# The expert stage of a float32 decoder: experts in an order found at run time, second blocks on resident weights, no loop, earlier turns of the activations

## The chip, the cores and the metric

The program runs on one core of one Trainium2 chip. The metric is the device time of one execution in microseconds (us). The profile is one execution, and all positions below are us from the start of its span.

## The reference, cut to what matters

The reference is a stack of two decoder blocks and a third one with a mixture of experts at its end. The change touches only that last part:

```python
logits = (xt @ router_w + router_b)            # 512 tokens, 32 experts
top_logits, top_idx = lax.top_k(logits, TOP_K) # 4 experts for each token
gates = jax.nn.softmax(top_logits, axis=-1)
# the tokens of each expert, in blocks of MOE_BLOCK rows:
hmid = xt[tok] @ w_gu[e] + b_gu[e]             # 1024 -> 2048, float32
glu  = jnp.minimum(hmid[:, 0::2], SWIGLU_LIMIT)
lin  = jnp.clip(hmid[:, 1::2], -SWIGLU_LIMIT, SWIGLU_LIMIT)
act  = glu * jax.nn.sigmoid(SWIGLU_ALPHA * glu) * (lin + 1.0)
out  = act @ w_down[e] + b_down[e]             # 1024 -> 1024
y = sum over the 4 chosen experts of gate * out
```

## The kernel before

Each expert has six units of weights of 2 MB: units 0 to 3 are the up weights, units 4 and 5 the down weights. They are loaded from HBM by SyncE's queue (L4183) into a ring of eight slots; a load waits until the unit that held the slot has been used (`unit_used`). So at most eight units, one expert and a third, are on the chip.

An expert's block holds up to 128 tokens, and a block is computed in one of two ways, chosen at run time by the number of its tokens (`is_half`):

- a **half block** (up to 64 tokens): float32 products in which two groups of 64 rows share the array (`up_half` L3698, `down_half` L3726). The activations are turned (transposed) by `turn_act_half` (L3711) once both pairs of up units are done, and `save_act_half` copies them from PSUM.
- a **full block** (65 to 128 tokens). Expert 0 has a plain float32 form for it (`up`, `down`). All others have the **parted** form: unit 0 in float32 (L3900), then each quarter of units 1 to 5 split by ScalarE into a rounded part (L88) and by VectorE into the rest (L91), and three products (L3870, L3871, L3875). `down_and_turn_parted` does unit 4, then turns the second half of the activations; `down_parted` does unit 5.

`first_blocks` walks the 32 experts in the order of their numbers. Experts 0 to 3 are written out, experts 4 to 27 are a loop of six iterations of four experts (`Fori`, on SyncE, TensorE, VectorE and ScalarE alike), and experts 28 to 31 are written out again. TensorE's instructions of one expert are: the up products, half of the turning of the next expert's rows (L3590), the turning of activations, the other half of the rows, the down products, and `find_tokens` of a later expert (L3559, the last instruction of each expert but the last three). Rows of an expert's tokens are fetched by GpSimd (L3575).

Tokens beyond the 128th of an expert are an **extra block**. `find` and `fill` work out on VectorE which there are (up to 15), and `extra_blocks` runs them after the 32 experts, in a loop of 15 iterations in each of which the body is behind an `If`. The weights of the first extra block's expert are loaded at the end of `first_blocks` (L4194), those of a later one in the body before it (L4351). The normed tokens are loaded whole (L4354), gathered by products with a selection matrix (L3665), and the block runs in either form. Last, `combine_and_finish` gathers each token's four rows (L4666), adds them and normalises.

Of the kernel before, what the change touches and what calls it, by code (L numbers as in the profile page):

```python
# [5 lines left out]
ALU = mybir.AluOpType  # L6
# [1015 lines left out]
def mlp(k, i, gain, clear_rows=False):  # L1022
# [15 lines left out]
    with ExitStack() as ctx:  # L1038
# [19 lines left out]
        with k.block() as block:  # L1058
# [35 lines left out]
            def _(act):  # L1094
                if clear_rows:
                    act.wait_ge(k.pool_made.sem, k.pool_made.at(1))
                for n, (u, is_up, j) in enumerate(order):
                    k.round_unit(act, u + 1)
                    if clear_rows:
                        rows = k.rows[3 * n:min(3 * n + 3, BLOCKS)].rearrange("b p d -> p b d")  # L1100
                        act.dma_start(rows, zero[:, :, :].broadcast_to([P, rows.shape[1], D])).then_inc(k.rows_cleared, 16)
# [2362 lines left out]
BLOCKS = EXPERTS + MOST_EXTRA  # L3464
# [3 lines left out]
SLOTS = 8  # L3468

# [32 lines left out]
class Experts:  # L3502


    def __init__(self, k, name, tables, one_by_one):
# [6 lines left out]
        self.loaded = [signal(f"loaded{r}") for r in range(SLOTS)]  # L3512
        self.sel_ready = signal("sel_ready")
        self.index_full = signal("index_full")
        self.index_ready = signal("index_ready")
        self.fetched = [signal(f"rows_fetched{r}") for r in range(2)]
# [16 lines left out]
    def make_sel(self, dve, j, par):  # L3533
# [4 lines left out]
        for t in range(TT):  # L3538
            ins = dve.tensor_scalar(T.sel[:, par, t, :], T.iota[:, :], T.place[:, t, bass.ds(j, 1)], None, ALU.is_equal)
# [95 lines left out]
    def save_act(self, act, j):  # L3635
        k, T = self.k, self.tables
        act.wait_ge(self.act_turned, 2 * j + 2)
        act.activation(T.actT[:, :, :].rearrange("p (b f) s -> p b (f s)", b=2), k.psum[:, 4:6, :], ACT.Copy)\
           .then_inc(self.actT_ready, 2)
# [33 lines left out]
    def up(self, pe, j, home, xg, par):  # L3673

        k, T = self.k, self.tables
        for pair in range(2):
            for r in range(2):
                w = home.wait(pe, 2 * pair + r)
                for g in range(2):
# [4 lines left out]
                    for c in range(HALF_K):  # L3684
                        pe.matmul(bank, xg[:, HALF_K * r + c, :], w[:, c, g * 512:(g + 1) * 512],
                                  start=(r == 0 and c == 0), stop=False)
# [20 lines left out]
    def turn_act_half(self, pe, j):  # L3707
        k, T = self.k, self.tables
        pe.wait_ge(self.act_ready, 4 * j + 4)
        for i in range(4):  # L3710
            ins = pe.transpose(k.psum[:, 4, i * P:(i + 1) * P], T.act[:, i * P:(i + 1) * P], k.ident[:, :])  # L3711
        ins.then_inc(self.act_turned, 2)

    def wait_for_down(self, pe, j):
        pe.wait_ge(self.actT_ready, 2 * j + 2)
# [3 lines left out]
    def down_half(self, pe, j, home, par, parted=False):  # L3719
        k, T = self.k, self.tables  # L3720
        self.wait_for_down(pe, j)
        w = [home.wait(pe, 4), home.wait(pe, 5)]
        banks = [k.psum[64 * g:64 * g + 64, 6, :] for g in range(2)]
        for c in range(KT):
            for g in range(2):
                ins = pe.matmul(banks[g], T.actT[:, c, 0:HALF], w[c // HALF_K][:, c % HALF_K, g * 512:(g + 1) * 512],  # L3726
                                start=(c == 0), stop=False)
        if parted:
            ins.then_inc(self.quarter_used.sem, 2 * HALF_K)
        for g in range(2):  # L3730
            pe.matmul(banks[g], T.bias_ones[:, par, 0:HALF], T.down_parts[:, g * 512:(g + 1) * 512], start=False,
                      stop=True).then_inc(self.down_full, 1)
# [18 lines left out]
    def sigmoids_half(self, act, j):  # L3751
        T = self.tables
# [3 lines left out]

    def save_act_half(self, act, j, parted=False):

        k, T = self.k, self.tables
        act.wait_ge(self.act_turned, 2 * j + 2)  # L3760
        turned = k.psum[:, 4, :].rearrange("p (pair h g s) -> p pair g h s", pair=2, h=2, g=2)
        home = T.actT[:, :, :].rearrange("p (pair g h) s -> p pair g h s", pair=2, g=2)
        ins = act.activation(home[:, 0, :, :, 0:HALF], turned[:, 0], ACT.Copy)
        if parted:
            ins.then_inc(k.unit_rounded.sem, PARTED + 1)
        act.activation(home[:, 1, :, :, 0:HALF], turned[:, 1], ACT.Copy).then_inc(self.actT_ready, 2)  # L3766
# [21 lines left out]
    def down(self, pe, j, home, par):  # L3788
# [953 lines left out]
```

## Time and the profile before

| what | us |
|---|---|
| median of the runs of before (3) | 3099.51 (3095.38 to 3104.8) |
| the profiled execution's own time | 3098.87 |
| its span | 3097.1 |
| first up product of expert 0 to last down product of expert 31 | 1894.2 to 2948.2 |
| from there to the first gather of the combination | 2948.2 to 3056.6 |
| combination and output | 3056.6 to 3097.1 |

The first 1894 us are the blocks ahead of the experts and are not touched by the change, but for a longer clearing of the output rows and some constants. The three last lines of the table are the stages that it touches. An engine's busy time is the sum of its instructions; "idle before ... <- X" is the time that it sat idle ahead of an instruction and what released it, where "issue" is a wait that the profile ascribes to nothing.

### The profile page before, as it was taken

The page shows a single profiled execution, that of the slowest core. Times are in us where ns is not written, and L with a number is a line of the kernel's source. Part 1 is how long each engine was busy: PE and PEld are TensorE (multiplying, and loading weights), DVE is VectorE, ACT ScalarE, POOL GpSimd, SP SyncE. Part 2 cuts the span into 40 slices and gives each one's busy share as a digit, 9 for nine tenths or more (in the row PEclk, how much of TensorE's full clock was granted, in tenths as well). Part 3 has the DMA queues.
Part 4 walks back from the last instruction along what each step waited for, and adds up shares of the span by engine and source line. Part 5 has one row for each costly group of instructions (what it writes and reads, how often), then busy time and mean ns, then how long its engine had stood idle before and what let it go on. Part 6 is the DMA issues. An engine that isn't in the chain of part 4 may idle for free. (4 is left out here: it accounts for less than half of the span.)

```text
span 3097.1 us, 35668 instructions
## 1 busy us (share of the span) xinstructions
PE 2741.5 (89%) x13162; PEld 1970.5 (64%) x13163; DVE 1614.4 (52%) x2447; ACT 1047.0 (34%) x1464; POOL 193.8 (6%) x213
## 2 busy tenths in 40 slices
PE   7877999999999899999966876998989998899962
PEld 6655778888878788888754663553655455455530
DVE  4864545444555544446855536652855454464413
ACT  4444443322224432233333231330634233343301
POOL 0530000000000000000012130000000000000002
PEclk9988999999999999999976787999999999999986
DMA  3110314444233132322210038999999999999974
GB/s 131 58 51 28 109 62 177 171 169 183 101 120 111 66 116 82 109 82 71 103 60 1 1 122 329 404 414 414 413 385 380 361 412 370 414 412 395 415 291 151
DMA packets 192096, 638.46 MB, mean 206 GB/s; under 512 B 12413, under 2 KB 18204, under 8 KB 191522
## 3 DMA queue, kind: packets, MB, share of 16 engines
q1 hardware_dynamic: 173856, 579.61, 48.7%
q10 hardware_dynamic: 11106, 39.11, 3.2%
q0 software_dynamic: 6912, 16.68, 1.4%
q8 instruction: 151, 2.47, 0.3%
q14 instruction: 71, 0.58, 0.1%
HBM read 600.61 MB, written 43.25 MB: 208 GB/s over the span
## 5 line engine op out<-in xcount | busy, mean ns | idle before, releaser
L91 DVE TENSOR_TENSOR unit_low<-unit_whole,unit_high 128x4096 fp32r<-128x4096 f32 (+3 forms) x95 | 287.8, 3035 | 174.8 <-ACT unit_high L88 172.9
L669 PE MATMUL psum<-tokens_high,unit_high 128*128 128x512 f32 (+2 forms) x1016 | 372.5, 367 | 4.4 <-PEq L865 1.6
L669 PE MATMUL psum<-tokens_high,unit_low 128*128 128x512 f32 (+2 forms) x1016 | 368.7, 363 | 0.0
L669 PE MATMUL psum<-tokens_low,unit_high 128*128 128x512 f32 (+2 forms) x1016 | 368.6, 363 | 0.0
L88 ACT ACTIVATE unit_high<-unit_whole 128x4096 fp32r<-128x4096 f32 (+2 forms) x65 | 225.8, 3474 | 374.2 <-PE psum L669 291.3
L91 DVE TENSOR_TENSOR moe_low<-ring_slot,moe_w_high 128x1024 fp32r<-128x1024 f32 x228 | 266.7, 1219 | 19.4 <-ACT moe_w_high L88 18.4
L88 ACT ACTIVATE moe_w_high<-ring_slot 128x1024 fp32r<-128x1024 f32 x228 | 236.5, 1055 | 61.4 <-PE psum L3875 60.4
L3698 PE MATMUL psum<-ring_slot,hT 128*64 128x512 f32 x1136 | 251.9, 594 | 0.0
L669 PEld LDWEIGHTS psum<-tokens_high,unit_high 128*128 128x128 f32 (+1 forms) x1016 | 191.0, 188 | 37.9 <-DVE unit_low L91 4.0
L669 PEld LDWEIGHTS psum<-tokens_low,unit_high 128*128 128x128 f32 (+1 forms) x1016 | 191.1, 188 | 31.6 <-issue 1.6
L669 PEld LDWEIGHTS psum<-tokens_high,unit_low 128*128 128x128 f32 (+1 forms) x1016 | 191.0, 188 | 30.6 <-issue 0.2
L669 PE MATMUL psum<-unit_high,hidden_high 128*128 128x512 f32 x512 | 199.7, 390 | 0.0
L669 PE MATMUL psum<-unit_high,hidden_low 128*128 128x512 f32 x512 | 199.4, 389 | 0.0
L669 PE MATMUL psum<-unit_low,hidden_high 128*128 128x512 f32 x512 | 199.4, 389 | 0.0
L3741 DVE TENSOR_SCALAR moe_glu<-psum 128x256 f32<-128x256 f32 x42 | 17.8, 425 | 324.4 <-PE psum L3704 232.7
L3698 PEld LDWEIGHTS psum<-ring_slot,hT 128*64 128x64 f32 x1136 | 83.5, 137 | 148.9 <-issue 147.7
L3726 PE MATMUL psum<-ring_slot,moe_actT 128*64 128x512 f32 x640 | 155.8, 641 | 9.7 <-ACT moe_actT L3766 9.7
L1147 DVE TENSOR_TENSOR x_residual<-psum,x_residual 128x512 f32<-128x512 f32 x128 | 84.4, 687 | 117.7 <-PE psum L669 117.7
L3870 PE MATMUL psum<-moe_w_high,moe_xg_high 128*128 128x512 f32 x312 | 131.1, 420 | 0.0
L3755 ACT ACTIVATE moe_sig<-moe_glu 128x256 f32<-128x256 f32 x42 | 17.5, 416 | 316.0 <-DVE moe_glu L3741 316.0
L3871 PE MATMUL psum<-moe_low,moe_xg_high 128*128 128x512 f32 x312 | 122.1, 391 | 0.0
L1137 DVE SCALAR_TENSOR_TENSOR hT<-psum,hidden_relu 128x512 f32<-128x512 f32 x64 | 43.8, 689 | 147.3 <-ACT hidden_relu L1109 147.3
(646 smaller groups left out, 4908.9 us busy)
## 6 DMA issues: line engine op xcount, KB each, us to landing
ring_slot<-in_moe_w_gu SPq DMA_DIRECT2D x118, 2048.0 KB, 19.4
ring_slot<-in_moe_w_down SPq DMA_DIRECT2D x60, 2048.0 KB, 20.5
unit_whole<-in_moe_w_gu SPq DMA_DIRECT2D x18, 2048.0 KB, 16.9
unit_whole<-in_w_up SPq DMA_DIRECT2D x16, 2048.0 KB, 7.5
unit_whole<-in_w_down SPq DMA_DIRECT2D x16, 2048.0 KB, 7.7
expert_rows<-zero_row ACTq DMA_DIRECT2D x15, 1536.0 KB, 5.3
unit_whole<-in_moe_w_down SPq DMA_DIRECT2D x8, 2048.0 KB, 19.7
unit_whole<-in_w_in SPq DMA_DIRECT2D x5, 2048.0 KB, 7.7
```

Of the source, the lines that this page charges most:

```text
L88: return act.activation(self.high, self.whole, ACT.Copy)
L91: return dve.tensor_tensor(self.low, self.whole, self.high.bitcast(F32), ALU.subtract)
L669: ins = pe.matmul(bank, a, c, start=(first and m == 0), stop=(last and m == len(parts) - 1))
L1137: dve.scalar_tensor_tensor(out=hidden[j % 2].whole[:, b, :], in0=bank, scalar=0.0, in1=relu[:, h % 2, :], op0=ALU.max, op1=ALU.mult)\
L1147: dve.tensor_tensor(x, bank, x, ALU.add).then_inc(k.bank_free.sem, 1)
L3698: ins = pe.matmul(banks[g], xg[:, c, 0:HALF], w[c // HALF_K][:, c % HALF_K, g * 512:(g + 1) * 512], start=(c == 0), stop=False)
L3726: ins = pe.matmul(banks[g], T.actT[:, c, 0:HALF], w[c // HALF_K][:, c % HALF_K, g * 512:(g + 1) * 512], start=(c == 0), stop=False)
L3741: dve.tensor_scalar(T.glu[:, pair, :], bank[:, :, 0], 7.0, None, ALU.min).then_inc(self.glu_ready, 2)
L3755: act.activation(T.sig[:, pair, :], T.glu[:, pair, :], ACT.Sigmoid, scale=1.702).then_inc(self.gate_ready, 2)
L3870: pe.matmul(banks[g], a.high[:, f, :], w.high[:, cols], start=(first and q == 0), stop=False)
L3871: pe.matmul(banks[g], a.high[:, f, :], w.low[:, cols], start=False, stop=False)
```

## The change

1. **An order found at run time.** `put_in_order` ranks the experts by their counts of tokens on VectorE: experts 0 and 1 stay first and second, the others are taken by `RANKS`, rank 0 being the most loaded one. There are 34 steps: expert 0, expert 1, rank 0, rank 0's second block, rank 26, then twelve pairs of ranks (2, 14), (3, 15) to (13, 25), then rank 1, rank 1's second block, and ranks 27, 28, 29.
2. **Second blocks with resident weights.** The two most loaded experts are computed twice in a row on one load of their weights (steps 2 and 3, steps 29 and 30). All four of these steps have, for a full block, the plain float32 form ("whole"). What is left over stays with `extra_blocks`, which now loads weights and tokens inside its body only.
3. **No loop.** All 34 steps are written out on every engine; an expert's number and the column of its places are read from a table into registers.
4. **Turns.** In a half block the first pair of activations is turned inside the second pair's up products and copied at once; the second pair is turned between the down products of unit 4 and of unit 5. In the parted form the second half is turned ahead of the last quarter of unit 4, not behind it. Both halves of the next expert's rows are turned together after the up products.

The diff's core:

```diff
+STEPS = EXPERTS + SECONDS            # 32 + 2
+AT_SECOND = (3, STEPS - 4)
+FIRST = 2
+RANKS = [EXPERTS - 2, EXPERTS - 1, 0, 0, 26] + [r for m in range(12) for r in (2 + m, 14 + m)] + [1, 1, 27, 28, 29]
+def in_steps(step):
+    for q, b, kind in ((0, 0, "first"), (1, 1, "parted"), (2, 2, "whole"), (3, 2, "whole"), (4, 3, "parted")):
+        step(Step(q, 0, b, kind))
+    for i in range(1, ROUND_LAST):
+        for b in range(PER_ROUND):
+            step(Step(PER_ROUND * i + b + 1, i, b, "parted"))
+    for q, b, kind in ((0, 0, "whole"), (1, 0, "whole"), (2, 1, "parted"), (3, 2, "parted"), (4, 3, "parted")):
+        step(Step(STEPS - 5 + q, ROUND_LAST, b, kind))
...
     def up_half(self, pe, j, home, xg, par, parted=False):
...
             for c in range(KT):
+                if pair == 1 and c == HALF_K:
+                    self.turn_act_half(pe, j, 0)
...
+        for pair in range(2):                       # down_half
+            if pair == 0:
+                self.wait_for_down(pe, j, 1)
+            else:
+                self.turn_act_half(pe, j, 1)
+                if finds:
+                    self.find_tokens(pe, j + 3, 1 - par)
+                pe.matmul(banks[0], T.bias_ones[:, par, 0:HALF], T.down_parts[:, 0:512], start=False, stop=False)
+                pe.wait_ge(self.actT_ready, 2 * j + 2)
...
     def down_and_turn_parted(self, pe, j, home):
...
-        self.unit_products(pe, j, 4, home, self.banks(6), self.tables.act_parts, True, self.act_low_at(j, 0))
+        self.unit_products(pe, j, 4, home, banks, parts, True, self.act_low_at(j, 0), range(HALF_K - 1))
         self.turn_act_pair(pe, j, 1)
+        self.unit_products(pe, j, 4, home, banks, parts, True, None, range(HALF_K - 1, HALF_K))
...
             for q in range(HALF_K):                 # activate_parted
+                if pair == 1 and q == HALF_K // 2:
+                    split_act(pair)
                 self.split_quarter(dve, j, n + 1, q, home)
-            split_act(pair)
+            if pair == 0:
+                split_act(pair)
...
+    def put_in_order(self, dve):
...
+        step(dve.tensor_tensor(more, keys.unsqueeze(1).broadcast_to([P, EXPERTS, EXPERTS]),
+                               keys.unsqueeze(2).broadcast_to([P, EXPERTS, EXPERTS]), ALU.is_gt))
+        step(dve.reduce_sum(T.rank[:, :], more, AX))
+        for i, of in enumerate((T.ids, T.counts)):
+            step(dve.tensor_tensor(here, T.rank[:, :].unsqueeze(1).broadcast_to([P, STEPS, EXPERTS]),
+                                   T.ranks[:, :].unsqueeze(2).broadcast_to([P, STEPS, EXPERTS]), ALU.is_equal))
+            step(dve.tensor_tensor(here, here, of[:, :].unsqueeze(1).broadcast_to([P, STEPS, EXPERTS]), ALU.mult))
+            step(dve.reduce_sum(T.by_step[:, i, :], here, AX))
...
+            def load(home, q, used_by):             # first_blocks, SyncE
+                e = expert_at(sp, q)
+                for n in range(PER_EXPERT):
+                    by = used_by[0 if n < 2 else 1]
+                    if by is not None:
+                        used(by, (n - 2) % PER_EXPERT)
+                    sp.dma_start(ring_view(k, home.slot(n)), expert_unit(k, e, n)).then_inc(E.loaded[home.slot(n)], 16)
...
+            load(Home(E, 0, 3), 4, (1, 3))
+            load(Home(E, 0, 4), 5, (3, 4))
...
             E.save_tokens(dve, 1)                   # first_blocks, VectorE
-            E.make_sel(dve, 2, 0)
             E.make_bias(dve, 0, 0)
+            E.make_bias(dve, 1, 1)
+            extras.put_in_order(dve)
             E.save_gather(dve, 0, 0, 0)
             E.save_gather(dve, 0, 1, 0)
+            E.make_sel(dve, 2, 0, column_at(dve, 2))
+            E.make_sel(dve, 3, 1, column_at(dve, 3))
             extras.find(dve)
             extras.find_jumps(dve)
-            in_rounds(dve, step)
+            in_steps(step)
...
             def body(b):                            # extra_blocks, SyncE
+                e = expert_of(sp, b)
+                sp.wait_ge(block_free, b + 1)
+                sp.dma_start(T.y, k.y_rows.rearrange("(t p) d -> p t d", p=P)).then_inc(y_loaded, 16)
+                for n in range(PER_EXPERT):
+                    sp.dma_start(ring_view(k, n), expert_unit(k, e, n)).then_inc(E.loaded[n], 16)
```

## Rows read from the trace of the kernel before

**Rows 1.** Two stages: length, PE, PEld, DVE, ACT, POOL busy, clock, DMA share, GB/s

```profile
1894.20:2948.20 1054.00, 972.05 (x4328) 541.18 (x4328) 566.20 (x913) 375.85 (x464) 32.56 (x30) 0.97 1.00 397
2948.20:3056.60 108.40, 64.36 (x342) 33.79 (x340) 11.40 (x30) 6.94 (x16) 0.00 (x0) 0.84 0.48 191
```

**Rows 2.** Timeline of TensorE, ScalarE and GpSimd after expert 31

```profile
2947.88 0.39 PE L3731 MATMUL psum<-moe_down_bias_parts,moe_bias_ones 128*64 128x512 bf16 x2
2969.85 9.18 PE L3665 MATMUL psum<-moe_sel_whole,ring_slot 128*128 128x128 f32 x64 [21.58 <-issue]
3043.73 0.38 PE L3731 MATMUL psum<-moe_down_bias_parts,moe_bias_ones 128*64 128x512 bf16 x2
3048.48 0.20 ACT L4407 ACTIVATE moe_store_seen<-ones 128x1 f32<-128x1 f32 x1 [3.09 <-DMA expert_rows<-moe_o]
3056.64 0.96 POOL L4666 DMA_INDIRECT unit_whole<-expert_rows,moe_row  x1 [189.49 <-PEq L4660]
```

**Rows 3.** DMA issues from 1780 on: KB each, median us to landing

```profile
ring_slot<-in_moe_w_down SPq DMA_DIRECT2D x60, 2048.0 KB, 20.5
unit_whole<-in_moe_w_down SPq DMA_DIRECT2D x8, 2048.0 KB, 19.7
expert_rows<-moe_o ACTq DMA_DIRECT2D x13, 512.0 KB, 7.8
expert_rows<-moe_o ACTq DMA_DIRECT2D x21, 256.0 KB, 6.3
```

**Rows 4.** Windows of four experts' steps (columns as in rows 1)

```profile
2046.40:2086.70 40.30, 38.45 (x164) 27.53 (x163) 32.40 (x39) 25.13 (x27) 1.23 (x1) 1.00 1.03 415
2855.70:2881.00 25.30, 23.36 (x120) 8.47 (x118) 4.78 (x13) 2.67 (x6) 0.99 (x1) 1.00 1.03 413
...
2278.50:2325.10 46.60, 40.95 (x164) 28.60 (x163) 32.62 (x39) 25.02 (x27) 1.23 (x1) 0.93 0.96 373
2391.00:2431.30 40.30, 38.44 (x164) 27.63 (x163) 32.63 (x39) 24.91 (x27) 1.23 (x1) 1.00 0.92 352
```

**Rows 5.** Waits of TensorE, 1890 to 2950: us in total, times, longest

```profile
PE psum L3711 <- DVE moe_act L3748: 32.3, 19, 2.7
PE psum L3875 <- DVE moe_actT_low L3944: 11.8, 13, 1.0
PE psum L3870 <- ACT moe_actT_high L3979: 11.7, 13, 0.9
...
PE psum L3900 <- issue: 11.2, 3, 3.8
PE psum L3726 <- ACT moe_actT L3766: 9.3, 18, 0.8
PE psum L3698 <- issue: 5.6, 2, 3.8
```

**Rows 6.** Timeline of TensorE: at a loop's edge, and between written-out experts

```profile
2282.42 9.64 PE L3900 MATMUL psum<-unit_whole,hT 128*128 128x512 f32 x16 [3.69 <-issue]
...
2881.10 7.13 PE L3900 MATMUL psum<-ring_slot,hT 128*128 128x512 f32 x16
```

**Rows 7.** Timeline of TensorE: first float32 unit of a full block

```profile
2046.51 7.11 PE L3900 MATMUL psum<-ring_slot,hT 128*128 128x512 f32 x16
2053.36 0.50 PE L3870 MATMUL psum<-moe_w_high,moe_xg_high 128*128 128x512 f32 x1
```

**Rows 8.** Timeline of VectorE around the first expert

```profile
1891.35 0.69 DVE L3605 TENSOR_TENSOR hT<-psum,feature_vectors 128x512 f32<-128x512 f32 x1 [11.19 <-PE psum L3590]
...
1894.74 1.66 DVE L4103 TENSOR_TENSOR extra_pick<-extra_order,moe_nth 128x1440 f32<-128x1440 f32 x1
...
1906.51 0.19 DVE L4131 TENSOR_TENSOR head_gains<-extra_order,moe_ids 128x32 f32<-128x32 f32 x1
...
1908.54 0.43 DVE L3741 TENSOR_SCALAR moe_glu<-psum 128x256 f32<-128x256 f32 x1 [1.13 <-issue]
...
1937.29 0.42 DVE L3741 TENSOR_SCALAR moe_glu<-psum 128x256 f32<-128x256 f32 x1 [0.86 <-DVE moe_row L4150]
```

More of the change, by code:

```diff
@@ L3796, in down @@
                 for c in range(HALF_K):
-                    pe.matmul(bank, T.actT[:, HALF_K * r + c, :], w[:, c, cols], start=(r == 0 and c == 0), stop=False)
+                    ins = pe.matmul(bank, T.actT[:, HALF_K * r + c, :], w[:, c, cols], start=(r == 0 and c == 0), stop=False)
+                if counted and r == 1 and half == 1:
+                    ins.then_inc(self.quarter_used.sem, 2 * HALF_K)
                 if r == 1:
@@ L4097, in find @@
         step(ins)
+        step(dve.scalar_tensor_tensor(out=self.flag[:, 0, :], in0=T.rank[:, :], scalar=float(SECONDS), in1=self.flag[:, 0, :],
+                                      op0=ALU.is_ge, op1=ALU.mult))
         dve.memset(self.zero[:, :], 0.0)
@@ L4204, in _, with step @@
             pool.wait_ge(T.y_stored, 16 * TT)
-            for j in range(EXPERTS):
-                E.fetch_rows(pool, j)
+            for q in range(STEPS):
+                E.fetch_rows(pool, q)
         @block.tensor
         def _(pe):
-            def step(i, b, j, first, last):
-                half = is_half(pe, j)
-                home = Home(E, i, b)
-                par = b % 2
+            def step(s):
+                if s.q == FIRST:
+                    pe.wait_ge(extras.ordered, 1)
+                half = is_half(pe, s)
+                q, home, par = s.q, s.home(E), s.par
@@ L4214, in step @@
                 xg = T.xg[:, par]
[L4215 to L4216 removed]
+                counted = s.kind != "first"
                 with pe.If(half):
[L4219 to L4220 removed]
+                    E.wait_for_up(pe, q)
+                    E.up_half(pe, q, home, xg, par, counted)
                 with pe.Else():
[L4222 to L4223 removed]
@@ L4226, in step @@
                 with pe.If(half):
-                    E.turn_act_half(pe, j)
+                    E.down_half(pe, q, home, par, counted, s.has(3))
                 with pe.Else():
-                    if parted:
-                        E.down_and_turn_parted(pe, j, home)
-                    else:
-                        E.turn_act(pe, j)
-                if following:
-                    E.turn_rows(pe, j + 1, 1, 1 - par, saved=j + 3 if not (last and b == PER_ROUND - 2) else EXPERTS)
-                with pe.If(half):
-                    E.down_half(pe, j, home, par, parted)
@@ L4237, in step @@
-                with pe.Else():
-                    if parted:
-                        E.down_parted(pe, j, home, par)
-                    else:
-                        E.down(pe, j, home, par)
-                if not (last and b >= 1):
-                    E.find_tokens(pe, j + 3, 1 - par)
+                    if s.kind == "parted":
+                        E.down_and_turn_parted(pe, q, home)
+                        E.down_parted(pe, q, home, par)
+                    else:
+                        E.turn_act(pe, q)
+                        E.down(pe, q, home, par, counted)
@@ L4295, in _, with step @@
+            extras.put_in_order(dve)
             E.save_gather(dve, 0, 0, 0)
             E.save_gather(dve, 0, 1, 0)
-            E.make_sel(dve, 3, 1)
-            E.make_bias(dve, 1, 1)
+            E.make_sel(dve, 2, 0, column_at(dve, 2))
+            E.make_sel(dve, 3, 1, column_at(dve, 3))
             extras.find(dve)
             extras.find_jumps(dve)
-            in_rounds(dve, step)
+            in_steps(step)
         @block.scalar
         def _(act):
-            def step(i, b, j, first, last):
-                parted = not (first and b == 0)
-                xg = T.xg[:, b % 2]
-                if first and b == 1:
+            def step(s):
+                q = s.q
+                if q == 1:
```

363 lines of the change are left out of this document (208 added, 155 removed).

## The prediction

> **What bounds the kernel now.** I read the windows first. From the first up product to the last down product the 32 experts take 1054.0 us, at 397 GB/s and a DMA share of 1.00; then the extra blocks take 108.4 us at 191 GB/s and half the DMA share [rows 1]. So there are two things to look at: a stage in which TensorE (972 us busy) and the DMA are both nearly full, and one in which neither is.
>
> The DMA issues tell how many blocks there are: 68 loads of down weights are 34 experts' loads, and the stores are 13 of 512 KB (full blocks) and 21 of 256 KB (half blocks), 34 blocks [rows 3]. So there are two extra blocks. Both are half: the down bias rows that close them and expert 31 are L3731, the half form [rows 2]. An expert with over 256 tokens would have a full extra block, so the two belong to two experts, each with 129 to 192 tokens: exactly the two that `AT_SECOND` takes. Of the 32 first blocks 13 are full and 19 half, experts 0 and 1 among the latter (L3741 is the half form) [rows 8]. By rank the full ones are 0 to 12.
>
> The single steps come next. A half block takes 25.3 us, of which TensorE is busy 23.4; a parted one 40.3, busy 38.5 [rows 4]. A load of an expert is 12.58 MB; where the DMA is full it moves 412 to 415 GB/s [rows 4], so 5.05 us for a unit and 30.3 for an expert. Half blocks are thus bounded by the DMA and parted ones by TensorE, and the ring evens out an expert and a third at most. In the same row list the step at 2391 moved only 352 GB/s: a parted block behind a parted one leaves the DMA idle. Last, the waits: TensorE waits in each half block for the activations (32.3 us in 19) and their copy (9.3), and in each parted one twice, 0.9 us each (11.7 and 11.8 in 13) [rows 5]. And it waits five times 3.4 us in mean (11.2 + 5.6), up to 3.8, for "issue" ahead of the first up product [rows 5], once at 2282.4, where sixteen products then take 9.64 us in place of 7.1 [rows 6, 7]. The five places are the experts 8, 12, 16, 20 and 24, the loop's back edges; the written-out experts (29 to 30, at 2881.10) have no such gap [rows 6].
>
> **The extra blocks go.** Both are done as second blocks, and the count of extra blocks becomes 0. From the last down product at 2948.2 the combination's first gather now comes 108.4 us later [rows 1]. What must stay: the copies and the store of the last block, some 5 us (3043.73 + 0.4 to 3048.48), and the walk through an empty loop; 13 empty iterations and the block's end take 8.2 us (3048.48 to 3056.64), so 15 take 9.4 [rows 2]. With 1.5 for two more block borders the tail is 16 us: **92 saved**. The reload of the residual, 2 MB or 5 us, lies beside it.
>
> **The start gets longer.** `put_in_order` stands on VectorE ahead of the first gather's copy. Two passes over 1024 elements and six over 1088: a pass over 1440 takes 1.66 [rows 8], so I scale to 1.22 and 1.29, together 10.2. Some eleven small ones of 0.1 to 0.2 and two register loads of 1.1 (the gap ahead of L3741 [rows 8]) make 14.4. VectorE idled 11.2 us there [rows 8]; less what is moved, the copy comes 2.5 late, and two register loads and the selections now behind it make the first up product 4.5 late. But VectorE is late from then on: `find` with six more small steps ends 7 us later, so the first activation comes at about 1915.4 and not at 1908.5. TensorE now stops for it in the middle of the second pair's up products (the new turn), and the half pair, activation, and down products still follow: step 0 ends 10 us later. The same again in step 1: `fill` and `find_rows` held the activation until 1937.3 [rows 8]; now until about 1950, and TensorE has 16 us of work left behind it. Step 2 starts at 1966 and not 1952: **14 lost**. If the pauses were hidden this would be 0; it can hardly be more than 20.
>
> **Shorter steps.** In a half block, turning the first pair inside the up products and the second between the down units takes away the two waits, (32.3 + 9.3) / 19 = 2.2 less some rest: 23.5. In a parted block the turned half has a quarter (1.4 us) to hide behind: 40.3 less 1.8 = 38.5. If nothing is won the steps stay 25.6 and 40.3. The back edges (five times 3.4 and up to 2.5 of slow products behind each [rows 6], together some 25 us) go.
>
> **Whole blocks.** Rank 0 and rank 1 lose the parted form. Sixteen records of float32 take 6.85 us (2046.51 to 2053.36) [rows 7], 0.43 each; a whole block has 64 up and 32 down, 41.1 us; six bias products 1.3, turns and tokens 2.0, the last activation, copy and borders 3.5: **48 us**, twice.
>
> **The pairs, and the DMA's holes.** A pair of a parted and a half step is 62 us for TensorE. For the DMA it is two loads, a store of 0.52 and one of 0.26 MB, and 0.6 MB of rows: 26.6 MB, or 64.2 us at 414 GB/s. So after the change the DMA is the bound of the pairs, and the shorter steps are worth little by themselves. And it gets two holes. The ring lets it bring two units of the next expert while a whole block runs (10 us), then nothing until the second block frees its first pair, 7 us into it. I walk it step by step:
> - step 2, 1966 to 2014; step 3 frees its first units at 2021. The DMA has been idle since about 1976.
> - from there the DMA is never without a free slot (I followed slots and landings for steps 3 to 9: each slot is free 3 to 10 us before the DMA comes to it). Until the second unit of step 29 it brings 150 units, 314.6 MB, with 6.3 of rows and 9.4 of stores 330 MB, **800 us** at 413. TensorE would need 16.4 + 23.5 + 11 x 38.5 + 13 x 23.5 = 769; it waits the other 31.
> - step 29 (whole), 2821 to 2869.
> - steps 30 to 33, half, 23.5 each and bound by the loads after the hole: units 2 to 5 of step 31 and twelve more from 7 us on, sixteen of 5.05 and the last down products, **97 us**. End of the last down product 2966.
>
> That is 18 later than 2948.2. With the tail of 16: the first gather at 2982 for 3056.6, **75 us** saved. On the profiled execution's 3098.87 (its span is 3097.1, and it stands 0.6 below the median of the runs shown) this gives 3024.
>
> **A rule on the DMA's rate.** The full windows moved at most 415 GB/s [rows 4]. The Trainium skill, page "DMA: Bandwidth & Descriptors", section "Bandwidth", has 425 GB/s for a 16 MB load; by that the long stretch would be 777 us in place of 800 and the sum 3001. No row here reaches it.
>
> **Rivals.**
> - *TensorE stays the bound: the turns win nothing.* For it: the waits may only move, to ScalarE's copy behind its roundings. Then steps 3 to 28 take 18 + 25.6 + 11 x 40.3 + 13 x 25.6 = 820 for 800, steps 31 to 33 another 2, and the time is 3046. Against: the waits lie where the change puts work, and VectorE is busy only 32 of 40 us in a parted step [rows 4].
> - *The order costs nothing* (VectorE's idle 11 us take it and TensorE's pauses shrink): 3010.
> - *The holes are wider*: the DMA also misses time in the pairs, or idle TensorE is granted a lower clock (0.93 in the step with a pause, 1.00 without [rows 4]) and a parted step takes 42 for 38.5. That would be up to 11 x 3.5 = 39 less the 31 of slack, and 2 us a pair of lost transfer on top: 3050 to 3080.
> - *Slower: the written-out steps stop as the back edges do.* Every step now jumps over the arm that it does not take. If that cost the 3.7 us of a back edge and the 2.5 of slow products behind it [rows 6], 34 steps cost 211, less the 31 of slack: 3204. It decides from 3.1 us a step on. Against: before, experts 0 to 3 and 28 to 31 jump over the same arms, with no gap [rows 6]. The Trainium skill, page "Runtime: NRT & Kernel Launch", section "Instruction fetch mechanics", says that a taken branch to outside the fetched window waits for a fetch; by that rule the back edges' gaps are explained, and the jumps would pay only if an arm were longer than the window.
> - *The change doesn't do what it says*: an extra block is left. The rows exclude it for these inputs.
>
> **How the numbers follow.** Forecast (3008 to 3040) 0.62; turns without gain (3040 to 3050) 0.14; order free and faster DMA (under 3008) 0.06; wider holes (3050 to 3080) 0.12; slower 0.04; the rest 0.02 near no change. The range reaches from 3008, the free order, to 3056, the turns without gain and some of the wider holes: about 0.8. A measurement of this kernel tells 0.3% (9 us) from no change. Faster 0.94, same 0.02, slower 0.04.
>
> **What would show it.** No product of the gather L3665 and no wait of 20 us ahead of the combination; 66 down loads become 64; VectorE's order for some 14 us before the first copy; step 2 at 1966; whole blocks of 48 us with the DMA idle for over 35 us in the first; pairs of 64 us at 412 to 415 GB/s, with half steps of 23.5 where nothing waits; no 3.7 us gaps. The prediction falls if the pairs take over 67 us, or the tail over 25.

## The result, and the profile after

| what | before, us | after, us |
|---|---|---|
| median (4 runs each) | 3098.27 (3095.38 to 3104.8) | 3062.72 (3055.36 to 3066.16) |
| profiled execution's own time, span | 3098.87, 3097.1 | 3055.36, 3053.3 |

The ratio is 0.9874 (0.9848 to 0.99): 35.6 us or 1.3% faster, where 3024 had been forecast with a range of 3008 to 3056. The direction was right, and the gain was half of what I had said. The profiled execution is the fastest of its four; it stands 31 us above the forecast, and the median another 7.4.

The windows of the changed kernel by stage: length, PE, PEld, DVE, ACT, POOL busy, clock, DMA share, GB/s (as [rows 1]):

```profile
1894.00:1961.00 67.00, 54.11 (x236) 21.76 (x236) 46.49 (x113) 5.76 (x12) 1.98 (x2) 0.89 0.83 325
1977.00:2017.20 40.20, 37.95 (x119) 16.62 (x119) 8.91 (x33) 3.11 (x6) 0.00 (x0) 0.96 0.04 15
2017.20:2838.70 821.50, 786.30 (x3521) 436.05 (x3517) 443.58 (x700) 319.43 (x401) 28.42 (x26) 0.99 1.02 408
2853.00:2895.00 42.00, 39.75 (x125) 17.42 (x125) 6.95 (x20) 3.53 (x7) 0.13 (x1) 0.96 0.27 105
2895.00:2991.20 96.20, 89.57 (x418) 37.13 (x414) 17.34 (x47) 10.33 (x26) 1.98 (x2) 0.98 0.90 361
2991.20:3013.30 22.10, 0.01 (x1) 0.00 (x0) 0.00 (x0) 1.39 (x3) 0.00 (x0) 0.58 0.32 109
```

The first row is steps 0 and 1. The second and fourth are the DMA's two holes, beside the two experts whose weights stay: TensorE is busy, the DMA moves 15 GB/s in the first and 105 in the second, which it fills for a quarter. Between them the DMA is full for 821.5 us. In the last row TensorE does nothing and the DMA brings 2.4 MB, the residual for the most part; this stage was 108.4 us before [rows 1].

The timeline of VectorE has the new order ahead of the first gather's copy (L3638), with two small gaps of "issue" where registers are loaded:

```profile
1877.38 1.23 DVE L4165 TENSOR_TENSOR extra_prod<-extra_order 128x1024 f32<-128x1024 f32 x1
1878.64 1.22 DVE L4167 TENSOR_REDUCE moe_rank<-extra_prod 128x32 f32<-128x1024 f32 x1
1879.89 1.29 DVE L4169 TENSOR_TENSOR extra_prod<-moe_rank,moe_ranks 128x1088 f32<-128x1088 f32 x1
...
1889.74 0.17 DVE L4187 TENSOR_SCALAR moe_place<-moe_place 128x4 f32 x1 [1.04 <-issue]
1890.49 0.17 DVE L4187 TENSOR_SCALAR moe_place<-moe_place 128x4 f32 x1 [0.57 <-issue]
1890.70 1.29 DVE L3638 TENSOR_TENSOR hT<-psum,feature_vectors 128x512 f32<-128x512 f32 x2
```

TensorE's timeline shows what that does: in steps 0 and 1 the turn of the first pair (L3751) stops for an activation that VectorE is late with. The third row is the start of step 2, the fourth that of step 29:

```profile
1912.91 0.69 PE L3751 MATMUL psum<-ident,moe_act 128*128 128x128 f32 x2 [5.74 <-DVE moe_act L3796]
1945.39 0.69 PE L3751 MATMUL psum<-ident,moe_act 128*128 128x128 f32 x2 [6.97 <-DVE moe_act L3796]
1961.13 10.57 PE L3721 MATMUL psum<-ring_slot,hT 128*128 128x512 f32 x24
...
2838.66 7.10 PE L3721 MATMUL psum<-unit_whole,hT 128*128 128x512 f32 x16 [0.61 <-issue]
```

SyncE's timeline has the holes: four loads whose issue takes 61.6 us because the last two wait for step 3 to free the first pair, and nothing between the loads at 2843.56 and at 2894.84:

```profile
1956.68 61.60 SPq L4295 DMA_DIRECT2D ring_slot<-in_moe_w_gu  x4
...
2843.56 9.15 SPq L4295 DMA_DIRECT2D ring_slot<-in_moe_w_gu  x2
2894.84 0.37 SPq L4295 DMA_DIRECT2D unit_whole<-in_moe_w_gu  x1
```

The end, on TensorE, ScalarE and GpSimd (as [rows 2]): last down product, store seen, first gather of the combination:

```profile
2990.83 0.38 PE L3780 MATMUL psum<-moe_down_bias_parts,moe_bias_ones 128*64 128x512 bf16 x1
2995.75 0.20 ACT L4519 ACTIVATE moe_store_seen<-ones 128x1 f32<-128x1 f32 x1 [3.23 <-DMA expert_rows<-moe_o]
3013.32 0.96 POOL L4779 DMA_INDIRECT unit_whole<-expert_rows,moe_row  x1 [90.47 <-PEq L4773]
```

The walk from 2995.75 to 3013.32 does no work at all: 15 rounds of the loop of extra blocks, each with nothing in it. It took 17.6 us, where 13 such rounds had taken 8.2 [rows 2].

And the rate of the long stretch, in three windows of 64 us of the same view:

```profile
2058.00:2122.00 64.00, 63.63 (x285) 36.47 (x283) 37.95 (x56) 28.80 (x36) 2.22 (x2) 1.00 1.03 414
2378.00:2442.00 64.00, 63.12 (x283) 36.40 (x285) 37.97 (x56) 28.45 (x36) 2.22 (x2) 1.00 1.02 409
2570.00:2634.00 64.00, 60.92 (x274) 35.49 (x270) 37.16 (x55) 28.05 (x34) 2.22 (x2) 1.00 1.02 405
```

At a full DMA share it falls from 414 to 405 GB/s. That was in no row of before on which I had built.

### The profile page after: what moved, and what is told of

Read it like the earlier page. It is cut to its first block and busy times, and to the rows that moved or that the text cites. A ratio compares the mean times of both kernels' runs of the same rounds, so it can differ in the third digit from the quotient of the medians.

```text
span 3053.3 us, 34265 instructions
## 1 busy us (share of the span) xinstructions
PE 2739.2 (90%) x12978; PEld 1934.9 (63%) x12979; DVE 1575.4 (52%) x2449; ACT 1011.2 (33%) x1445; POOL 196.6 (6%) x249
## 5 line engine op out<-in xcount | busy, mean ns | idle before, releaser
L3738 PE MATMUL psum<-ring_slot,hT 128*64 128x512 f32 x1184 | 274.6, 611 | 15.3 <-DMA ring_slot<-in_moe_w_gu 15.3
L91 DVE TENSOR_TENSOR moe_low<-ring_slot,moe_w_high 128x1024 fp32r<-128x1024 f32 x200 | 233.2, 1218 | 4.0 <-ACT moe_w_high L88 3.9
L88 ACT ACTIVATE moe_w_high<-ring_slot 128x1024 fp32r<-128x1024 f32 x200 | 208.2, 1057 | 44.0 <-PE psum L3922 42.7
L3789 DVE TENSOR_SCALAR moe_glu<-psum 128x256 f32<-128x256 f32 x42 | 17.8, 425 | 354.7 <-PE psum L3744 259.3
L3738 PEld LDWEIGHTS psum<-ring_slot,hT 128*64 128x64 f32 x1184 | 95.6, 140 | 163.2 <-issue 151.1
L3774 PE MATMUL psum<-ring_slot,moe_actT 128*64 128x512 f32 x624 | 145.9, 610 | 16.3 <-issue 14.7
L3917 PE MATMUL psum<-moe_w_high,moe_xg_high 128*128 128x512 f32 x264 | 108.2, 410 | 2.9 <-DVE moe_low L91 2.8
L660 PE MATMUL psum<-unit_high,high_parts 128*128 128x512 f32 (+2 forms) x256 | 99.5, 389 | 10.5 <-DVE low_parts L1997 4.1
L669 PEld LDWEIGHTS psum<-unit_high,hidden_high 128*128 128x128 f32 x512 | 96.1, 188 | 19.9
## 6 DMA issues: line engine op xcount, KB each, us to landing
unit_whole<-in_moe_w_gu SPq DMA_DIRECT2D x16, 2048.0 KB, 24.3
```

What stands on the lines that cost most here:

```text
L88: return act.activation(self.high, self.whole, ACT.Copy)
L91: return dve.tensor_tensor(self.low, self.whole, self.high.bitcast(F32), ALU.subtract)
L660: ins = pe.matmul(bank, a, c, start=(i == 0 and m == 0), stop=(i == len(products) - 1 and m == len(parts) - 1))
L669: ins = pe.matmul(bank, a, c, start=(first and m == 0), stop=(last and m == len(parts) - 1))
L3738: ins = pe.matmul(banks[g], xg[:, c, 0:HALF], w[c // HALF_K][:, c % HALF_K, g * 512:(g + 1) * 512], start=(c == 0), stop=False)
L3774: ins = pe.matmul(banks[g], T.actT[:, HALF_K * pair + c, 0:HALF], w[pair][:, c, g * 512:(g + 1) * 512], start=(pair == 0 and c == 0), stop ...
```

## The experiments

All are edits of the changed kernel. "H" in an expectation is the theory that the DMA and its holes set the pace, "P" the rival that TensorE's steps do. Medians are of 4 to 10 executions. Executions of the same code differ by 10 to 15 us (3055.36 to 3066.16 for the changed kernel, 3052.13 to 3067.38 in run 11), so beside the medians I compare positions in the profiles, above all that of the last down product: 2990.83 in the first profile of the changed kernel, 2995.58 in its second (run 11).

**1. The place of the second hole's weights.** The two blocks of each of the two most loaded experts change places: the half-full second block comes first, and the full one behind it, now in the parted form, which frees its units one by one.

```diff
-AT_SECOND = (3, STEPS - 4)
+AT_SECOND = (2, STEPS - 5)
...
-(3, 2, "whole")    # and (1, 0, "whole") at the end
+(3, 2, "parted")   # and (1, 0, "parted")
```

> The changed kernel with the two blocks of the most loaded experts in the other order: the second block (half) first, then the first block, which can then take the parted form and frees its units one after another. Theory H (the stage goes at the pace of the DMA, plus the time in which no slot is free): the time without transfers behind step 2 falls from some 40 us to 15 and that behind step 29 from some 31 to 5, so about 50 us less than the changed kernel's 3063: 3012. Rival P (TensorE's steps set the pace): only the two whole blocks become parted ones, 2 x (49 - 38.6) = 21 less: 3042.

Measured: 3028.02, ratio 0.9769 (0.9748 to 0.9791), 35 us less than the change as made. That lies in the middle between H (3012) and P (3042) and decides for neither. SyncE's timeline does more. The four loads at the first hole are now issued in 42.4 us in place of 61.6, and at the second hole no load is issued for 23.9 us (2835.54 to 2859.45) in place of 42.1:

```profile
1957.27 42.40 SPq L4295 DMA_DIRECT2D ring_slot<-in_moe_w_gu  x4
...
2825.76 9.78 SPq L4295 DMA_DIRECT2D ring_slot<-in_moe_w_gu  x2
2859.45 0.37 SPq L4295 DMA_DIRECT2D unit_whole<-in_moe_w_gu  x1
```

Of the 19.2 us at the first hole 17.8 are kept at the loads ahead of the second (2825.76 for 2843.56): this hole was paid almost in full, though TensorE is busy beside it, as H has it; P would give some 10. The last down product comes at 2963.58 for 2990.83, 27.3 us earlier, so of the 18.2 us at the second hole only some 9.5 are kept. That is what P gives for one block (48.8 - 38.6): behind it the last three half steps take 72.9 us in place of 79.6, 24.3 each, TensorE's own pace. The median's 35 holds besides the 7.4 us by which the changed kernel's median stands above its profiled execution.

**2. The order.** Parted experts first, then the half ones.

```diff
-+ [r for m in range(12) for r in (2 + m, 14 + m)] +
++ list(range(2, 26)) +
```

> The changed kernel with the 24 middle steps sorted by count (eleven parted ones, then thirteen half ones) and not paired. Theory H: in each parted step behind a parted one the DMA idles some 5 us, and the half steps then run at the DMA's pace of 32 us each; the stretch takes about 11 x 38.6 + 13 x 32 = 841 against 785 for the same steps paired: 50 us more, 3113. Rival P: the sum of TensorE's steps is the same, so 3063.

Measured: 3094.72, ratio 0.9986 (0.9972 to 1.0001): 32 us worse than in pairs. Its windows say why. With parted steps alone TensorE has not one idle us and the DMA brings 354 GB/s; with half steps alone TensorE is busy 207 of 256 us, at 412:

```profile
2186.00:2442.00 256.00, 256.00 (x1099) 185.94 (x1098) 218.64 (x266) 166.70 (x182) 8.59 (x7) 1.00 0.97 354
2570.00:2826.00 256.00, 207.28 (x944) 76.53 (x942) 44.83 (x136) 23.01 (x56) 7.91 (x8) 0.95 1.02 412
```

The pairing is thus worth about as much as the whole change. The parted steps also show that a DMA share near 1 (0.97) does not mean a full rate: with 354 GB/s the engines count as busy.

**3. Fewer bytes.** In steps 4 to 28 only one row of each block is stored; 9.4 MB of stores are left out, and the output lacks those rows.

```diff
-dma_start(self.rows_of(block, HALF), T.o[0:HALF, :])
+dma_start(self.rows_of(block, 1 if few else HALF), T.o[0:1 if few else HALF, :])
```

> The changed kernel storing only one row of each block in steps 4 to 28 (it leaves out the rest of these stores, 9.4 MB). Theory H: 9.4 MB at 408 GB/s are 23 us less, 3040; and if the stores are also what takes the rate from 414 to 405 GB/s in the later pairs, another 12 less, 3028, with 414 in all windows. Rival P: nothing changes, 3063.

Measured: 3035.56, ratio 0.9802 (0.9777 to 0.9827): 27 us less, 26 of them in steps 2 to 28 of the profile (851.6 us for 877.5). At 413 GB/s the bytes are 23. No work of TensorE was taken away, so with the new turns the DMA is the bound of the stretch. Its rate still fell, to 404 to 410 from 2378 on: the stores are not the cause of the fall.

**4. The old turns.** Turning of activations as before, in both forms; the edit puts back the old `down_half`, `turn_act_half` and `down_and_turn_parted`, and the copies and splits that go with them.

```diff
-                if pair == 1 and c == HALF_K:
-                    self.turn_act_half(pe, j, 0)
...
-        self.unit_products(pe, j, 4, home, banks, parts, True, self.act_low_at(j, 0), range(HALF_K - 1))
+        self.unit_products(pe, j, 4, home, self.banks(6), self.tables.act_parts, True, self.act_low_at(j, 0))
         self.turn_act_pair(pe, j, 1)
-        self.unit_products(pe, j, 4, home, banks, parts, True, None, range(HALF_K - 1, HALF_K))
```

> The changed kernel with the turns of the activations and of the next rows where the kernel before had them. Theory H: the shorter steps lie inside the DMA's pace; only steps 0, 1, 3, 4 and 30 to 33 show them, a few us, and steps 0 and 1 no longer stop in the middle of the up products: 3060 to 3072. Rival P: eleven parted steps of +1.8 and twenty half steps of +2 us: +60, 3120.

Measured: 3065.91, ratio 0.9885 (0.9861 to 0.9909): 3 us above the change, which is within the scatter. But that is a difference of two larger ones. With the old turns step 2 starts at 1954.74, 6.4 us before that of the changed kernel (1961.13; 11.8 before its second profile), and step 29 at 2848.32, 9.7 us behind it (2838.66):

```profile
2848.32 7.11 PE L3721 MATMUL psum<-unit_whole,hT 128*128 128x512 f32 x16
```

So steps 2 to 28 take 893.6 us in place of 877.5 (875.0 in the second profile), 16 to 19 more, and the DMA's rate over the long stretch is 400 GB/s and not 408: TensorE was the slower of the two there. The new turns save this time and give back 6 to 12 us of it at the start, where the turn inside the up products waits for a late VectorE. TensorE's waits in the long stretch, first with the old turns, then in the changed kernel:

```profile
PE psum L3749 <- DVE moe_act L3786: 23.5, 15, 1.6
PE psum L3915 <- DVE moe_actT_low L3984: 10.9, 11, 1.0
PE psum L3910 <- ACT moe_actT_high L4019: 8.4, 11, 0.8
PE psum L3764 <- ACT moe_actT L3804: 4.7, 14, 0.4
```

```profile
PE psum L3774 <- issue: 17.0, 9, 3.0
PE psum L3738 <- DMA ring_slot<-in_moe_w_gu: 11.0, 5, 3.3
PE psum L3917 <- DVE moe_low L91: 2.8, 8, 0.7
```

47.5 us of waits for turned activations are gone, and 31 of other waits have come. 11.0 of them are for weights by name. The 17.0 of "issue" at L3774, ahead of the first down product of a half step, have no releaser in the trace. They are likely waits for the down weights: with fewer bytes (run 3) 3.5 us of them are left, and no half step before 2233 has one, though each has the same jump. That was not shown further.

**5. The start.** `find` and `fill` are spread over VectorE's time in steps 0 to 2, and `find_rows` over steps 4 to 10.

```diff
-            extras.find(dve)          # ahead of step 0
-            extras.find_jumps(dve)
...
+                    extras.find(dve)                      # after step 0
+                elif s.q == 1:
+                    extras.find_jumps(dve)
+                    extras.fill(dve, 0)
+                    extras.fill(dve, 1)
```

> The changed kernel with the search for extra blocks taken off the start: find after step 0, find_jumps and half of fill after step 1, the rest after step 2, find_rows in steps 4, 6, 8 and 10. If VectorE's lateness in steps 0 and 1 is what costs there (TensorE stops 5.7 and 7.0 us in the middle of the up products), step 2 starts at 1948 and not at 1961, and 13 us are kept to the end: 3050. Rival: the first weights arrive no sooner (units 2 to 5 of step 1 and of step 2 wait for used units anyway), and less than 4 us are won.

Measured: 3044.8, ratio 0.9827 (0.9806 to 0.9848): 18 us less. Step 2 starts at 1944.61 in place of 1961.13, 16.5 us earlier, and the DMA's first hole ends as much earlier (2001.75 for 2018.28). At the last down product 11.4 are left (2979.45 for 2990.83; 16.1 against the second profile), so most of it reaches the end, not all. The edit also gives step 1 the whole form for a full block; expert 1 has a half block and doesn't take that arm.

**6. The empty loop.** It is put behind one test of its count.

```diff
-            with eng.Fori(0, MOST_EXTRA) as b:
-                with eng.If(b < count):
-                    body(b)
+            with eng.If(count > 0):
+                with eng.Fori(0, MOST_EXTRA) as b:
+                    ...
```

> The changed kernel with the whole loop over extra blocks behind one more If on their count. The tail was forecast at 16 us and took 22.1. If it is the walk through fifteen empty iterations (some 1.1 us each), it falls to about 7 and the time by 15: 3048. Rival: it is the borders of the blocks and the store, and 3 us at most are won.

Measured: 3044.33, ratio 0.9819 (0.9797 to 0.9841): 18 us less. From the store seen to the first gather it is now 7.3 us, 10.3 less than in the first profile of the changed kernel and 17.8 less than in its second:

```profile
3000.59 0.20 ACT L4520 ACTIVATE moe_store_seen<-ones 128x1 f32<-128x1 f32 x1 [3.20 <-DMA expert_rows<-moe_o]
...
3007.85 0.96 POOL L4780 DMA_INDIRECT unit_whole<-expert_rows,moe_row  x1 [81.93 <-PEq L4774]
```

**7. The loop again.** Steps 5 to 28 as a loop of six iterations of four steps, on all four engines.

```diff
-    for i in range(1, ROUND_LAST):
+    with eng.Fori(1, ROUND_LAST) as i:
```

> The changed kernel with its steps 5 to 28 as a loop of six iterations again, on all four engines. Theory H: five back edges of some 6 us on TensorE lie within the DMA's pace for the most part (TensorE had 20 to 30 us of slack over the stretch): 3063 to 3073. Rival P: they add in full, 27 to 30 us: 3091.

Measured: 3087.48, ratio 0.9968 (0.9955 to 0.998): 25 us worse. My theory, that the DMA's slack takes the back edges, fell. TensorE waits five times for some 10 us at the back edges, with slow products behind (8.7 to 10.0 us for sixteen in place of 7.1), and five times for 1.0 to 1.3 us ahead of the parted step between:

```profile
2200.47 9.98 PE L3948 MATMUL psum<-unit_whole,hT 128*128 128x512 f32 x16 [10.37 <-issue]
```

```profile
PE psum L3948 <- issue: 56.4, 10, 10.4
```

The slow products are TensorE's clock: from 2200.5 to 2204 the granted clock is 0.50, the lower of its two levels (1.2 and 2.4 GHz), after 10 us in which it did nothing; from 2210 on it is 1.00 again. The 9.64 us of [rows 6] are the same, 0.50 from 2282.5 to 2286.5. 56.4 us of stops cost 25. Before, five such places had 16.8 in all [rows 5]; why a back edge takes 10 us in this loop of four steps and took 3.7 in that of four experts [rows 6], no run tells.

**8. The three together** (1, 5 and 6).

> Second block ahead of the first (as in the run before), late find and skipped empty loop together. By theory H they add up, since each takes away a time in which nothing is transferred: 3028 - 13 - 15 = 3000.

Measured: 3004.67 (3003.43 to 3005.08), ratio 0.9695 (0.9674 to 0.9716). It is 58 us below the change as made and beats both kernels. Alone they gave 35, 18 and 18, which is 13 more. In the profiles there is no overlap: the last down product comes 27.3 and 11.4 us earlier in runs 1 and 5 and 39.5 in this one (2951.33), and the walk through the empty loop falls from 17.6 to 6.8. The 13 fit the scatter: each single gain is counted from a median that stands 7.4 above the profiled execution, three times in the sum and once in the 58, which makes 15.

**9 to 11. Where the rate falls.** One kernel reads the weights of one expert for all steps but the first (the products are then with expert 5's weights); one takes the pairs in reverse; one is the changed kernel once more.

```diff
-                e = expert_at(sp, q)
+                e = 5
```

```diff
-[r for m in range(12) for r in (2 + m, 14 + m)]
+[r for m in range(12) for r in (13 - m, 25 - m)]
```

> The changed kernel with every weight load of the 34 steps reading the same expert's weights (expert 5), so all loads read one 12 MB stretch; each expert's tokens are multiplied by expert 5's weights, so the output is another one. Question: from about 2378 us on, the changed kernel's transfers moved 404 to 409 GB/s at a DMA share of 1.02, where the first five windows of 64 us moved 413 to 415. Theory A (the place read in memory: some experts' weights are read slower): all windows read alike, 412 to 415 throughout or one low value throughout; at 414 the long stretch of 821 us takes 12 us less and the median is about 3050. Theory B (what is mixed with the loads at that time, or the time in the run): the fall stays in the same windows, and the median is within 4 us of 3063.

> The changed kernel with its twelve pairs of parted and half steps taken in reverse, ranks 13 and 25 first and ranks 2 and 14 last; the same bytes and the same products. Theory A (the place read): the slow windows, 404 to 409 GB/s, move to the front of the stretch, 2058 to about 2500, and 413 to 415 come last; median within 4 us of 3063. Theory B (time or neighbours in time): 413 to 415 stay first, 404 to 409 stay last; the same median. The order of the pairs itself is worth nothing by either, since each pair moves 24 MB and needs 63 us of products.

> The changed kernel unaltered, once more, to stand beside the two others on the same chip and to give its windows a second time. Expected: a median within 4 us of 3062.7, and the fall of the rate from 413 to 415 down to 404 to 409 GB/s in the same windows, from about 2378 us on; if the fall is a chance of one execution, the windows differ by more than 3 GB/s from the first profile.

Measured: 3055.71, ratio 0.9867 (0.9846 to 0.9888); 3057.69, 0.9868 (0.9852 to 0.9885); 3061.07, 0.9868 (0.9847 to 0.9889). The fall is in the same windows in all three, from 2378 on (410 from 2314 on with the reversed pairs): 402 to 411 GB/s, 413 to 415 before but for 412 in one. The window from 2570 on:

```profile
2570.00:2634.00 64.00, 60.33 (x269) 35.59 (x272) 37.49 (x55) 28.05 (x34) 2.21 (x2) 1.00 1.02 405
```

```profile
2570.00:2634.00 64.00, 61.85 (x271) 35.80 (x270) 36.52 (x51) 28.06 (x34) 2.21 (x2) 0.98 1.02 404
```

The first is of the one expert, the second of the reversed pairs. Neither the place read nor the order is the cause. Loads that wait for a free slot are not the cause either: in the changed kernel the up units took 24.5 to 25.5 us from issue to landing in the windows from 2058 to 2186, and 24.2 to 26.0 from 2378 to 2698; where the queue runs short it is some 10 (the parted steps of run 2). The profile of the kernel run once more differs from the first in two places: the last down product comes 4.8 us later, and the walk through the empty loop took 25.1 us and not 17.6:

```profile
3000.53 0.20 ACT L4519 ACTIVATE moe_store_seen<-ones 128x1 f32<-128x1 f32 x1 [3.26 <-DMA expert_rows<-moe_o]
...
3025.63 0.96 POOL L4779 DMA_INDIRECT unit_whole<-expert_rows,moe_row  x1 [100.00 <-PEq L4773]
```

**12. A pause.** SyncE waits twice, ahead of the loads of steps 14 and 22, until the load before has landed.

```diff
+                    if b == 0 and i in (3, 5):
+                        Home(E, i, 0).wait(sp, PER_EXPERT - 1)
                     load(Home(E, i, b + 1), ...)
```

> The changed kernel, where SyncE waits twice, ahead of the loads of steps 14 and 22 (about 2330 and 2590 us), until the load before them has landed, so that the queue of loads runs empty once and then fills again with all freed units at once. Theory C (the rate of the loads falls with how long the queue has been full without a break, as the 16 DMA engines drift apart, and a pause sets it back): one slice of low rate at each place, then 413 to 415 GB/s for the next 200 us or more; each pause costs about 2 to 3 us of transfers and the higher rate gives back about 2% of 250 us, so that the median is 0 to 8 us below 3061. Theory B2 (the rate falls with the time in the run, whatever the queue did before): 404 to 409 GB/s in the windows from 2442 us on in spite of the pauses, and the median 2 to 10 us above 3061.

Measured: 3063.53, ratio 0.9883 (0.9859 to 0.9906). The rate is back at once, in the windows behind each pause:

```profile
2314.00:2378.00 64.00, 59.23 (x259) 34.62 (x257) 35.96 (x50) 27.58 (x32) 2.22 (x2) 0.97 0.89 348
2378.00:2442.00 64.00, 61.65 (x278) 35.72 (x276) 38.86 (x59) 28.03 (x34) 2.21 (x2) 1.00 1.03 415
...
2570.00:2634.00 64.00, 57.34 (x248) 34.01 (x248) 37.51 (x55) 27.65 (x33) 2.22 (x2) 0.96 0.90 356
2634.00:2698.00 64.00, 61.74 (x266) 35.76 (x264) 36.45 (x51) 27.65 (x33) 1.23 (x1) 0.96 1.03 413
```

So the rate depends on how long the queue has been full without a break, and not on the time in the run. The price of a pause was mis-sized: not 2 to 3 us of transfers but (414 - 348) / 414 and (414 - 356) / 414 of 64 us, 10 and 9. The shape of a draining queue hints at a cause. It stands in 40 slices of the DMA's busy tenths: the changed kernel at its first hole (slices of 1 us), behind steps 0 and 1 in which it was not full (share 0.83), the kernel with pauses (slices of 1.6 us), after some 300 us at full share, and the changed kernel at its second hole (slices of 1 us), after 821.5 us at full share:

```profile
DMA  9999999999999999970310000000000000000000
```

```profile
DMA  9999999999987536310199999999999999999999
```

```profile
DMA  9999999999842221100000000000000000000007
```

The first queue ends within 4 us, the second fades over some 11, the third over some 8. One reading is that the 16 DMA engines drift apart, and that a load counts as landed only when the last one has done its part. It stays a guess: the engines were not measured one by one, the fade after 821.5 us is no longer than that after 300, and fewer loads stood in the first queue (landing 15.2 us after issue, for some 25 in the others), which is a rival that no run separates. The pauses gave back 13 to 16 of their 19 us (step 29 comes at 2845.1, for 2838.7 and 2841.6 in the two profiles of the changed kernel) and won nothing in the median.

## Why the prediction was wrong in size, point by point

Against the profiled execution (31 us off) and with what the others showed:

- **Extra blocks go, 92 saved: right in kind, the tail mis-sized.** The tail is 22.1 us and not 16. The failing step was "15 take 9.4": I scaled the walk through the empty loop from 13 rounds behind the last full one. It measured 17.6 in this execution and 25.1 in the second profile, 7.3 with the loop skipped. In the eleven profiles that have this loop it is either 17.6 to 18.8 (seven) or 24.9 to 25.1 (four), so the tail is 6 or 14 us over my figure.
- **The start, 14 lost: right, 9 to 15 measured.** Step 2 at 1961.1 and 1966.6 in the two profiles, for 1966, by the mechanism named (the first turn stops for a late activation). Run 4 parts it: with the order but the old turns step 2 comes at 1954.7, so the order costs some 3 us and the turn inside the up products the rest. What I had not said is that it could be undone: run 5 moved VectorE's search and won 11 to 16 us at the last down product, 18 in the median.
- **Shorter steps: right on the steps, and the rival priced well what they bring.** Steps 3, 4 and 5 take 24.0, 24.1 and 38.6 us, for 23.5 and 38.5. The rival in which the turns win nothing set steps 3 to 28 at 20 us more; the old turns took 16 to 19 more in steps 2 to 28 (run 4). The 3 us of run 4's median are what is left after the loss at the start. That the shorter steps are "worth little by themselves" was too low.
- **Whole blocks, 48: right.** 1961.1 to 2010.1 is 49.0; step 29 took 48.8.
- **The holes: right in size, the first paid almost in full, the second for half.** The DMA stands nearly still from 1977 to 2017.2, and no load is issued for 42 us at the second. Run 1 shortened them by 19.2 and 18.2 us and kept 17.8 and 9.5.
- **The long stretch, 800 us: the step that failed most, 21.5 us.** "At 413" was the rate of windows behind pauses; the mean of the unbroken stretch was 408, which is 10 us. Before, the loop's edges and parted steps in a row (373 and 352 GB/s [rows 4]) had let the queue run short again and again, so its rows never showed the low rate of a queue that stays full. The rest is bytes: the DMA moved 335.6 MB for the 330 that I counted. 3.3 MB of the difference are weights (317.9 for 314.6, units under way at the window's end), 0.8 rows (7.1 for 6.3), and 1.2 are instructions, which I had left out. The Trainium skill, page "DMA: Bandwidth & Descriptors", section "Bandwidth", gives 425 GB/s for a 16 MB load; by that the stretch would have been still shorter. The trace disagrees twice, with 415 at most and 404 in the lowest window.
- **The last four steps, 97: 103.7.** I counted sixteen units of 5.05 and left out the rows and stores beside them: 34.7 MB went in that window, 84 us at 413 and not 81, and the ring's start gave 365 GB/s for 16 us.
- **Back edges: the slack was overrated.** My forecast took 31 us of slack in TensorE for granted. Run 7 lost 25 of 56. TensorE was busy 786.3 of the 821.5 us. That a stop of 10 us in one place costs more than a mean slack tells is my explanation, and no run tests it. The Trainium skill, page "Runtime: NRT & Kernel Launch", section "Instruction fetch mechanics", says that a taken branch to outside the fetched window waits for a fetch. The written-out steps with their jumps show one wait for "issue" ahead of a parted step's first product in the long stretch, of 2.7 us, and nine of 0.45 to 3.0 ahead of a half step's down products (run 4), and neither comes at every jump, so the rival that had a stop in every step (3204) did not come. The back edges of run 7 agree with the rule in kind.
- **Execution to execution.** The forecast stood on one profiled execution. That of the changed kernel has the short walk; the median of its runs lies 7 above. Its second profile has 7.5 us more of walk and 4.8 more before it; half of that would be 6.

In sum, in us against the forecast: start -5, stretch +21.5, whole blocks +1.8, last four steps +6.7, tail +6: 31, and 7 for the median.

## What to carry to other kernels

When a stage is at its DMA bound, ask of every edit first what it does to the time in which the queue is empty: shortening two holes beside busy TensorE work, by exchanging which of two blocks frees its weights first, won 27 us in the profiles (35 in the medians) with a few constants, where all shortened steps gave 16 to 19 in the long stretch. An edit whose median moves little can still hold a gain and a loss: compare the stages, not only the end. A rate taken from windows between pauses is too high for a stretch without any; take it from the longest full stretch that the trace has, and widen the range where there is none. Work that was made empty (a loop with a count of 0) still has its walk, so price it by a run or skip it by one test.

## What the runs showed of the hardware

- The rate of 2 MB loads at an unbroken DMA share of 1.02 fell from 412 to 415 GB/s to between 402 and 411 after some 300 to 360 us, in the changed kernel and with other reads, stores and orders (runs 3 and 9 to 11), and a pause of the queue brought 413 to 415 back (run 12).
- A round of an empty loop took (17.6 - 7.3) / 15 = 0.7 us in some executions and (25.1 - 7.3) / 15 = 1.2 in others; of eleven profiles none lies between 18.8 and 24.9 for the whole walk.
- A loop's back edge stopped TensorE for 10 us in one loop (run 7) and for up to 3.8 in another of the same number of steps [rows 5].
- After a stop of 10 us (run 7) or of 3.7 (the kernel before, at 2282.4) TensorE's granted clock was 0.50 for some 4 us, and sixteen products took up to 10.0 us in place of 7.1.
